# A hybrid encoder block on eight cores: weight loads, sine tables, copies back and norms in another order at the start, and a planner with another model of the queues

## What is computed

```python
h = rmsnorm(x, g_mix)
bc, cc, vc, q, k, va, gc_pre, ga_pre = split(h @ w_in)
y_c = (bc * causal_conv3(cc * vc)) @ w_conv_out
q, k = rope(rmsnorm(q)), rope(rmsnorm(k))
w = softmax(q0 k0 / 8) - lam * softmax(q1 k1 / 8)      # chunk-causal mask, chunks of 64
y_a = (rmsnorm(w @ va) * (1 - lam_init)) @ w_attn_out
x = x + (sigmoid(gc_pre + b) * y_c + sigmoid(ga_pre + b) * y_a) @ w_o
gt, up = split(rmsnorm(x, g_ffn) @ w_gate_up)
x = x + (silu(gt) * up) @ w_down
```

## Time and profile before

| | |
|---|---|
| median of three runs | 2176.37 us (2174.57 to 2176.63) |
| the profiled execution, its own time | 2176.54 us |
| its span on the slowest core (core 0) | 2174.6 us |
| spans of the other cores | 2169.9 to 2173.8 us |
| TensorE matmuls busy | 2135.9 us (98%) |
| VectorE, ScalarE, GpSimd busy | 971.5, 993.3, 408.2 us |
| moved by DMA | 330.97 MB, mean 152 GB/s |

### The profile page before, as it was taken

The page is one execution under the profiler, slowest core; times in us unless marked ns, Lnnn a source line. Parts: engine busy times, 40 slices in busy tenths (PEclk is TensorE's granted clock), DMA queues, the critical chain, the costliest instruction groups (busy, mean ns, idle before and its releaser), DMA issues.

```text
span 2174.6 us, 42940 instructions; the slowest of 8 cores (2169.9 to 2174.6 us)
## 1 busy us (share of the span) xinstructions
PE 2135.9 (98%) x16416; PEld 1289.3 (59%) x16416; DVE 971.5 (45%) x1866; ACT 993.3 (46%) x1545; POOL 408.2 (19%) x488
## 2 busy tenths in 40 slices
PE   6999999999999999999999999999999999999999
PEld 4455444578556585555855558556586565675547
DVE  5874644362465325643256431454323463213532
ACT  4566321123644425445354454644547545557210
POOL 4951110051232003310033000232001220001000
PEclk9999999999999999999999999999999999999999
DMA  9594696547546347553575533745328453252343
GB/s 235 121 208 116 148 218 154 129 103 222 171 126 186 113 143 226 171 152 105 154 215 165 143 104 120 230 123 178 107 79 253 126 166 109 91 184 81 120 171 119
DMA packets 163797, 330.97 MB, mean 152 GB/s; under 512 B 86672, under 2 KB 87568, under 8 KB 163344
## 3 DMA queue, kind: packets, MB, share of 16 engines
q1 hardware_dynamic: 154672, 296.25, 43.7%
q0 software_dynamic: 8928, 31.99, 9.4%
HBM read 291.48 MB, written 49.81 MB: 157 GB/s over the span
## 4 chain that ended last, share of the span: by engine, by line
PE 94%; DVE 2%; DMA 1%; POOL 1%; issue 1%; ACT 1%; SPq 0%; DVEq 0%; POOLq 0%; ACTq 0%
PE psB L1066 28%; PE psB L922 18%; PE psB L1100 14%; PE psO L829 11%; PE psB L796 7%; PE psB L997 5%; PE psB L1038 4%; PE psB L676 4%; PE psB L757 3%; DMA xt<-x 1%; DMA wring<-wblk 0%; PE psB L612 0%; DMA wsc<-wring 0%; DVE h L616 0%; POOL st L705 0%
## 5 line engine op out<-in xcount | busy, mean ns | idle before, releaser
L807 ACT ACTIVATE Pb<-psB 128x1024 bf16<-128x1024 f32 (+1 forms) x544 | 514.3, 995 | 480.9 <-PE psB L796 480.5
L1066 PE MATMUL psB<-h,wring 128*128 128x512 bf16 (+1 forms) x3040 | 625.9, 364 | 2.0 <-DVE kT L1079 1.3
L1066 PEld LDWEIGHTS psB<-h,wring 128*128 128x128 bf16 x3040 | 289.7, 98 | 308.6 <-issue 21.4
L922 PE MATMUL psB<-h,wring 128*128 128x512 bf16 x1792 | 416.9, 381 | 1.9 <-DVE scr L964 1.4
L829 PEld LDWEIGHTS psO<-Vs,Pb 128*128 128x128 bf16 x4224 | 263.5, 98 | 58.9 <-issue 7.8
L829 PE MATMUL psO<-Vs,Pb 128*128 128x129 bf16 x4224 | 290.4, 220 | 2.7 <-ACT Pb L807 2.7
L922 PEld LDWEIGHTS psB<-h,wring 128*128 128x128 bf16 x1792 | 166.6, 98 | 202.7 <-issue 22.3
L1100 PE MATMUL psB<-wring,big 128*128 128x256 bf16 x2464 | 281.4, 273 | 1.9 <-DVE big L1079 1.0
L1075 DVE SCALAR_TENSOR_TENSOR scr<-scr,psB 128x512 f32<-128x512 f32 (+1 forms) x190 | 123.1, 648 | 347.9 <-ACT scr L1073 347.6
L1100 PEld LDWEIGHTS psB<-wring,big 128*128 128x128 bf16 x2464 | 235.7, 98 | 42.2 <-issue 15.1
L1073 ACT ACTIVATE scr<-psB 128x512 f32<-128x512 f32 (+1 forms) x190 | 107.5, 566 | 235.3 <-PE psB L1066 230.8
(11 more groups left out here) (118 smaller groups left out, 1740.5 us busy)
## 6 DMA issues: line engine op xcount, KB each, us to landing
wring<-wsc SPq DMA_DIRECT2D x348, 512.0 KB, 4.3
wring<-wblk POOLq DMA_DIRECT2D x58, 512.0 KB, 8.8
wsc<-wring SPq DMA_DIRECT2D x58, 512.0 KB, 5.3
xt<-x SPq DMA_DIRECT2D x56, 512.0 KB, 7.3
out<-xt SPq DMA_DIRECT2D x28, 512.0 KB, 5.1
wring<-wsc SPq DMA_DIRECT2D x24, 384.0 KB, 3.5
Vs<-x SPq DMA_DIRECT2D x4, 512.0 KB, 20.2
qT<-x SPq DMA_DIRECT2D x4, 512.0 KB, 13.7
```

What stands on the lines that cost most here:

```text
L807: return act_ns(2 * w), [(lambda: A.activation(out=Pb[:, P.slot, :, 0:w], in_=psB[:, a:a + 2, 0:w], func=AF.Exp, scale=0.125), [(S2[0], 0) ...
L922: subs.append((lambda kc=kc: PEE.matmul(bank(B), lhsT=wring[:, W.slot, :].rearrange("p (k c) -> p k c", k=8)[:, kc, col * 128:(col + 1) * ...
L1066: subs.append((lambda kc=kc, gu=gu, B=B: PEE.matmul(bank(B)[:, 0:n], lhsT=wring[:, W.slot, :].rearrange("p (k c) -> p k c", k=8)[:, kc, gu ...
```

## The change

- **Opening.** The first weight block has no wait; the second waits for x's second row block (GATES). The list is V of tile 0, two conv units, V of tile 1 with Q of tile 0 woven into its second half, then the rest of conv with K of tile 0, Q and K of tile 1. So the weight order is V, V, one conv block, Q, Q, and on. Only tile 1's third x load, not its first, waits for the second V block.
- **Tables.** The first table step and the small constants read tile 0's fourth h (`behind`), so VectorE does them after tile 0's norms. The store to `csd` is moved to the first gate unit (soft).
- **Copies back.** Those of the first five blocks come, in the planner's play, after tile 1's fourth x load is in.
- **Tile 2.** Its Squares come, in the planner's play, after activation 18 of tile 1's FFN.
- **PSUM.** psO and psB are one tensor of eight banks. Attention uses banks 6 and 7 where it used psO; bank 6 goes to the free banks when the last attention unit is through.
- **Attention.** `attention` is now `attention_h`; a second form, `attention_q`, by quarters of a tile, is called for tiles from JH = 8 on, which there are none of. The planner's rule for pairs leaves out the condition on P.
- **Planner.** The two DMA queues share the rate 0.35 to 0.65 while both hold work, recomputed at each issue and landing; rate and latency are other constants; a gate unit waits when fewer than two scratch buffers are free, unless it is first in line.

```diff
-LASTW = 0.7
+LASTW, NEARLY = 0.7, 7
+JH, GROUP, FREE, LEAVE = 8, 3, 6, 3
+GATES = {1: (1,)}
...
-    DMA_LAT = 2600.0
+    DMA_RATE = 300.0
+    DMA_LAT = 2200.0
...
+        def rates():
+            both = queue["sp"] and queue["pool"]
+            return {e: self.DMA_RATE * ((0.35 if e == "sp" else 0.65) if both else 1.0) for e in queue}
+
+        def flow(at):
+
+            nonlocal asof
+            r = rates()
+            for e, q in queue.items():
+                if q:
+                    q[0][1] -= r[e] * (at - asof)
+            asof = at
+            for e, q in queue.items():
+                while q and q[0][1] <= 1.0:
+                    t = q.pop(0)[0]
+                    t.land = end = at + self.DMA_LAT
+                    for s in t.succ:
+                        if s.after is not t:
+                            push(end + self.SEM, "dep", s)
+                    for v in t.vals:
+                        push(end + self.SEM, "rel", v)
+
+        def plan_next(at):
+            nonlocal version
+            version += 1
+            r = rates()
+            ends = [q[0][1] / r[e] for e, q in queue.items() if q]
+            if ends:
+                push(at + max(min(ends), 0.01), "flow", version)
 
...
-                            if spare < 3:
+                            if spare < (t.visit[2] if last_kind == "qk" else 3):
                                 continue
                             if last_kind != "qk" and t.next is not None:
                                 t.first = now if t.first is None else t.first
-                                if (spare < 5 or len(self.pools["P"]) < 2 or t.next.ndep > 1) and now < t.first + t.patience:
+                                u, n = t, 1
+                                while n < t.visit[0] and u.next is not None and u.next.ndep <= 1:
+                                    u, n = u.next, n + 1
+                                if (spare < t.visit[1] or n < t.visit[0]) and now < t.first + t.patience:
                                     continue
+                        if t.kind == "gate" and len(self.pools["scr"]) < 2 and t is not line[head]:
+                            continue
...
-                        other = max(f for q, f in dma_free.items() if q != e)
-                        begin = max(dma_free[e], end)
-                        part = self.DMA_RATE * (0.35 if e == "sp" else 0.65)
-                        got = min(t.dma, max(0.0, (other - begin)) * part)
-                        dma_free[e] = begin + got / part + (t.dma - got) / self.DMA_RATE
-                        end = dma_free[e] + self.DMA_LAT
+                        push(end, "issue", t)
+                        for s in t.succ:
+                            if s.after is t:
+                                push(end, "dep", s)
+                        continue
...
-        psO = es.enter_context(nc.psum_tensor("psO", [128, 2, 512], F32))
-        psB = es.enter_context(nc.psum_tensor("psB", [128, NBANK, 512], F32))
+        psB = es.enter_context(nc.psum_tensor("psB", [128, 8, 512], F32))
...
+            behind = [(H[0], 3)]
...
             dve(1250.0, lambda: V.tensor_tensor(
                 out=setup_f, in0=pos_sb[:].unsqueeze(2).to_broadcast([128, 32, 32]),
-                in1=inv.unsqueeze(1).to_broadcast([128, 32, 32]), op=ALU.mult), [C("pos"), C("cst")], KF, pos)
+                in1=inv.unsqueeze(1).to_broadcast([128, 32, 32]), op=ALU.mult), [C("pos"), C("cst")] + behind, KF, pos)
...
-            dma(lambda: nc.sync.dma_start(out=cs_d, in_=cs_all.rearrange("p j s c -> p j (s c)")), VSET, [(CSD, 0)],
-                1048576, pos, lambda: "csd")
...
+        early = []
+
+        def write_back(b, v, n, pos, soft=()):
             dma(lambda: nc.sync.dma_start(out=wsc_d[b][:, 0:n], in_=wring[:, v.slot, 0:n]), [(v, 0)], [(WSC, b)],
-                256 * n, pos + 60000.0, lambda: ("cv", v.slot))
+                256 * n, pos + 60000.0, lambda: ("cv", v.slot), soft=soft)
 
         def weight(p, b):
             if (p, b) in wcur:
                 return wcur[(p, b)]
             v = val("ring")
-            gate = [0] if not wcur else []
+            gate = GATES.get(len(wcur), ())
             wcur[(p, b)] = v
             pos = clk["p"] - 40000.0
             n = 1536 if b in SHORT else 2048
             if p == 0:
                 dma(lambda: nc.gpsimd.dma_start(out=wring[:, v.slot, 0:n], in_=wblk_d[b][:, 0:n]), [(H[0].xs[g], 0) for g in gate], [(v, 0)],
                     512 * n, pos, lambda: ("wc", v.slot), q="pool", strict="w")
-                if b not in HB_AO:
+                if len(wcur) <= NEARLY and b in HB_V + HB_Q + (HB_CONV + 1,):
+                    early.append((b, v, n, pos))
+                elif b not in HB_AO:
                     write_back(b, v, n, pos)
...
-        def norm(X, t, dst, g, pos, pe=True):
+        def norm(X, t, dst, g, pos, pe=True, soft=()):
             XN, SM = val("xn"), val("sm")
-            act(act_ns(1024) + 190.0, lambda: A.activation(out=xn[:, XN.slot, :], in_=xv(X), func=AF.Square,
-                                                           accum_out=sm[:, SM.slot, 0:1]),
-                xk(X), [(XN, 0), (SM, 0)], pos)
+            pl.add("act", act_ns(1024) + 190.0, [(lambda: A.activation(
+                out=xn[:, XN.slot, :], in_=xv(X), func=AF.Square, accum_out=sm[:, SM.slot, 0:1]),
...
-                first = [(weight(0, b), 0) for b in HB_V][1:] if j == 1 and t == 0 else []
+                first = [(weight(0, b), 0) for b in HB_V][1:] if j == 1 and t == 2 else []
                 x_load(X, j, t, pos + step * t - 30000.0, reads=first)
-                norm(X, t, H[j], 0, pos + step * t, j < TN)
+                norm(X, t, H[j], 0, pos + step * t, j < TN, soft)
 
...
+        B6 = pl.val("bank", 6)
+
+        def OB(O, n):
+            return (O, 0) if n else (B6, 0)
...
+                pl.add("pe", w / 512.0 * MM + 15.0, subs, at, hold=False, strict="qk", kind="qk").visit = (2, 5, 3)
...
+        def attention_q(j):
...
+        def attention(j):
+            return attention_h(j) if j < JH else attention_q(j)
...
-        weave(v0 + q0 + v1 + conv0[:4] + conv1[:4], k0 + q1, 16)
-        weave(conv0[4:6] + conv1[4:6] + twins(conv0[6:], conv1[6:], 2), k1, 0, 6)
+        weave(v0 + conv0[:2] + v1 + conv1[:2], q0, 12)
+        for e in early:
+            write_back(*e, soft=[(H[1].xs[3], 0)])
+        weave(conv0[2:6] + conv1[2:6] + twins(conv0[6:], conv1[6:], 2), k0 + q1 + k1, 0, 12)
         a = clk["p"] - 12000.0
         mix0, mix1 = {}, {}
         weave(twins(gate_list(0, 0, HB_GC, HB_CO, by0, mix0), gate_list(1, 0, HB_GC, HB_CO, by1, mix1)), [])
+        dma(lambda: nc.sync.dma_start(out=cs_d, in_=cs_all.rearrange("p j s c -> p j (s c)")), VSET, [(CSD, 0)],
+            1048576, clk["p"] - 10000.0, lambda: "csd", soft=[(mix0[0], 0)])
         dma(lambda: nc.sync.dma_start(out=gb[:], in_=gb_d), [(mix0[0], 0)], [C("gb")], 1048576, clk["p"], lambda: "gb")
...
-        norm_in(2, clk["p"] + 10000.0, 2000.0)
+        norm_in(2, clk["p"] + 10000.0, 2000.0, [(act1[18], 0)])
```

More of the change, by code:

```diff
@@ L1 @@
 import contextlib
+import itertools
 import math
@@ L193, in order @@
         free_at = {e: 0.0 for e in ready}
-        dma_free = {"sp": 0.0, "pool": 0.0}
         now = 0.0
@@ L280, in order @@
                     if t.dma is not None:
-                        other = max(f for q, f in dma_free.items() if q != e)
-                        begin = max(dma_free[e], end)
-                        part = self.DMA_RATE * (0.35 if e == "sp" else 0.65)
-                        got = min(t.dma, max(0.0, (other - begin)) * part)
-                        dma_free[e] = begin + got / part + (t.dma - got) / self.DMA_RATE
-                        end = dma_free[e] + self.DMA_LAT
+                        push(end, "issue", t)
[3 more added lines that the diff above has]
+                        continue
                     for s in t.succ:
-                        if s.after is t and t.dma is not None:
-                            at = now + cost
-                        elif t.eng == "pe" and s.eng == "pe":
+                        if t.eng == "pe" and s.eng == "pe":
                             at = end
@@ L304, in order @@
             while True:
-                if what == "dep":
+                if what == "issue":
+                    flow(now)
+                    queue[x.eng].append([x, float(x.dma)])
+                    plan_next(now)
+                elif what == "flow":
+                    if x == version:
+                        flow(now)
+                        plan_next(now)
+                elif what == "dep":
                     x.ndep -= 1
@@ L627, in build_program, with norm_in @@
         H, HF, QT, TAB, ON = {}, {}, {}, {}, {}
-        def norm_in(j, pos, step):
+        def norm_in(j, pos, step, soft=()):
             H[j] = val("h8")
@@ L801, in qk_exp @@
                 w = 384 if last else 512
```

(4 more changed lines are left out.)

139 lines of the change are left out of this document (124 added, 15 removed).

## The result

| | before | changed |
|---|---|---|
| median of ten runs each | 2176.5 us | 2181.03 us |
| ratio, with its 95% interval | | 1.0024 (1.0014 to 1.0033) |
| the profiled execution, its own time | 2176.54 us | 2183.13 us |
| spans of the eight cores, lowest, median, highest | 2169.9, 2171.8, 2174.6 | 2172.0, 2175.8, 2181.5 |

The change makes the kernel slower by 0.24%, some 5 us; faster had been forecast, by 7.8. The ratios leave disturbed runs out, the medians do not; where both stand, the ratio counts.

The account below looks back on a forecast made before the run. TensorE, busy 2135.9 of 2174.6 us, was taken as the bound, with DMA transfers limiting the opening. Terms −4.8 and −3.0 summed to −7.8, so 2176.54 would become 2168.7 us, range 2161 to 2177.

Parts of the forecast that it names:

- term A: Opening, first V unit: tile 0's V done at about 25 instead of 29.8; −4.8 us, from −6 to −1.5.
- rival 1: Opening: the early weight takes the x blocks' bandwidth, gain falls to −1.5, time 2172.0 us; chance 0.09.
- term B: 30 to 62 us: half of the 5.8 us gaps, which hang on tile 1's norms, go; −3.0, from −7 to +2.
- Tables: Sine table steps from about 20 us: they fit beside the V units; nothing, up to +1 us.
- the rule set against them: Table steps beside tile 1's norms: two-port VectorE steps lock GpSimd out, up to 1.3 us in all; sum left unchanged.
- term C: 62 to 125 us: closer Q/K load on GpSimd set against tile 2's tables not made here; 0, from −3 to +3.
- The lower clock: 30 to 62 us: the 1.2 GHz stretch may not come with fewer gaps, or come elsewhere; no separate size given.
- D1: Held copies back, SP's queue and ring: the copies are hidden behind other work; 0.
- rival 3: Opening: held copies close the ring, the eighth weight block comes late, 15 us of stall, 2183.7 us; chance 0.08.
- D2: Planner's new queue model and rules may change later orders a little; pairs should stay pairs.
- Rival 4: QK pairs in attention: 70 more splits at 0.17 us each cost 12 us, time 2181; chance 0.04.
- Rival 2: Up to 125 us: GpSimd and VectorE are the limit, all but 2 us given back, 2174.5 us; chance 0.09.

Follow-up runs that it names:

- e11: Kernel before with the new weight requests and x loads, the planner's new pair and gate-unit rules and later tile 2 Squares; rest as before: ratio 1.0009.
- e4: Changed kernel with first weight block again behind x's first row block, second free, tile 1's first x load behind the second V block: ratio 1.0067.
- e3: Changed kernel with both the old opening list of units and the old place of the sine table steps: ratio 1.0022.
- e2: Changed kernel with the sine table steps free to run before tile 0's fourth h, as before: ratio 1.0011.
- e1: Changed kernel with the old opening list of units put back, all else as changed: ratio 1.0050.
- e7: Changed kernel, same queue order, VectorE's two rotation products for tiles 0 and 1 cut from 512 to 64 elements: ratio 1.0014.
- e10: Changed kernel, same queue order, with the cuts of e7 and e9 together: ratio 0.9986.
- e15: Changed kernel with tile 2's sines copied on chip by ScalarE (as e14) and the sine table steps in their old place: ratio 1.0002.
- e9: Changed kernel, same queue order, GpSimd's tile 2 table steps read a constant instead of waiting for the table read-back: ratio 1.0017.
- e14: Changed kernel, complete, with tile 2's sines copied on chip by ScalarE instead of read back from the scratch: ratio 1.0017.
- e12: Changed kernel with the planner's old model of the DMA queues (rate 290, latency 2.6 us, one share value): ratio 1.0044.
- e16: Changed kernel with tile 2's sines copied on chip, the sine table steps in their old place and the old opening list: ratio 1.0008.

## Why the prediction was wrong, step by step

- **First V unit (term A, −4.8, bounds −6 to −1.5): −1.6.** The step "nearer to the fastest: I take 11.5" failed. The norm came as worked out (10.28 for 10.2), the weight did not: 12.3 us from issue to use, more than the 10.6 of the median and than its "whole old delay" of 10.5, though nothing else was on its queue until 9.2. And "what follows must hold it" failed with it: x's third block landed 4 us later, and its Square stood another 2 us behind V's copy in ScalarE's queue. The first part is rival 1, which had −1.5 here: the early weight takes x's bandwidth. The Trainium skill (DMA: Bandwidth & Descriptors, "Queues, rings and completion order") says that the engines alternate between the queues packet by packet. By that rule the early weight and x's blocks share the engines, and the landings agree (12.1 us for x's third block, not 8.1). In e11, with the old list, the first 30 us won nothing at all.
- **30 to 62 (term B, −3.0): −2.5.** The size was right, and tile 1's last Square came at 39.37 instead of 44.19, as worked out. It takes all parts together: without the new requests it is at 50.21 (e4), with them but without the held copies at 47.67 (e11), in the runs with both between 38.6 and 41.5. And with the old list the stretch still has 5.3 us idle (e3), 2.9 of them before a transpose of Q. The text had the list as a cost here; it carried part of the gain.
- **Tables (0 to +1): some 3 us.** In idle time it is 1.4 us in 30 to 62 (e2 against the changed kernel). But e2 has the same idle time up to 240 in sum (28.3 and 28.2) and a price of the clock of 1.7 where the changed kernel has 5.1, and it is faster by 0.0013, 2.8 us (the two intervals overlap). The five steps fit beside the V units as said, but they end at 39.4 and GpSimd's table steps after them, and in e1 Q waited for that. Of the rule set against them, one case shows: the power that GpSimd began at 26.29, beside the first table step (26.18), took 1.53 us, where the one at 6.45 took 0.56.
- **62 to 125 (term C, 0): +3.8 of idle.** This is the step that gave the gain back: all kernels with the new list and no work left out have 7.6 to 9.3 us here, where before has 3.9. The text had both halves of it: GpSimd at 92% (57.54 of 63 are 91%), and Q and K "closer together". It then set a favour against them, that tile 2's tables can't be made here. The favour was small (GpSimd 54.2 instead of 57.5 busy), and the load was not GpSimd's alone. Of 63 us, VectorE has 51 and GpSimd 54 in a chain that passes from one to the other and back; sixteen units in 72 us instead of 82 leave it no slack. The square of e1 to e3 shows that this idle time goes with the list, e7 and e10 that it hangs on the chain.
- **The lower clock** was named for 30 to 62 only as something that may go ("it may not come, or come elsewhere"). It came elsewhere: 0.92 in 62 to 125 on core 7, and it had no place in the sum. By the table's account it is most of what makes the change slower and not equal: up to 240 us the idle time is 28.2 in sum against 27.3 before, while the price of the clock is 5.1 against 1.7. It follows the gaps only loosely: e2 and e15 have 8.1 and 8.0 us idle in 62 to 125 and a price of 1.7.
- **The store of the tables (favour of term C; D1: 0): 1.5 us in the changed kernel** (e9 and e14), 2 and 3 us in e2 and e3. The step read the moved store as work taken out of a full stretch. It did not follow the read-back: a DMA of 128 KB that takes 13 us to be of use, and GpSimd's queue behind it.
- **Copies, ring, rival 3 (slower, 0.08): did not happen.** The eighth weight was asked for at 46.80, as predicted (before 48). The ring was no cause.
- **Planner, tile 2's Squares (D2, 0, −3 to +4): +0.8** in 240 to 2150. e12 is slower, so the new queue model is not the cause, and e11, which has the later Squares and the new rule for pairs, has 7.7 there. Rival 4 (split pairs) did not happen either: 24 visits of four QK matmuls before, 26 after, not 70 more. That its 2181 is the measured time is chance.
- **Rival 2 (0.09)** had the mechanism, "earlier matmuls only wait longer in term C", and gave back all but 2 us. What it lacked is that the give-back could exceed the gain: by the clock, and by a second stall further on. No case had that, so nothing above 2177 was in the range but by a mishap. The likeliest case should have been that one: with 98% busy TensorE, and VectorE plus GpSimd at 80 to 90% right behind the opening, a shorter opening was by these rows more likely to be given back than kept.

What stays open: where the +0.8 after 240 comes from, and why gaps of the same sum cost 1.7 us of clock in e2 and 5.1 in the changed kernel. And whether Q and K units begun at 30, as before, with the new gates' x loads, can keep the 2.5 us of 30 to 62: the planner's orders tried (e3, e16, e11) did not.

## What to carry to other kernels

A gap closed ahead of a stretch in which two helper engines are over 80% busy only moves, so cost the next stretch as a chain: number of units, first and last start, time for each. When a store moves later, follow its reader: what waits for the read-back, and what is queued behind that wait. And on eight cores, where the slowest sets the time, allow for a gap to be paid twice where the profile shows TensorE at its lower clock after such gaps.

## What the runs showed that was not expected

- A weight block alone on its queue took 12.3 us from issue to use (2.10 to 14.44), more than the first of the four issued together before (10.5, from 5.36 to its copy back at 15.87).
- A read of 128 KB took 12.9 us (147.37 to 160.23) in one kernel and 13.1 in another (143.02 to 156.11), with the DMA engines busy to 0.94 and 0.89 of these stretches.
- Gaps of 2 to 3 us in TensorE's work were followed by stretches at 1.2 GHz on some cores and not on others of the same run (the price was 1.7 us on cores 0, 2 and 4 of the changed kernel, 3.4 on core 6 and 6.8 on cores 1, 3, 5 and 7). In e10, where the gap of 106 to 110 was gone and 1.8 us of that of 80 to 84 left, none of the eight cores had one in 62 to 125.
- Taking away VectorE work alone, with every queue's order kept, made the kernel before faster by some 3 us. The Q and K chain was a limit in a kernel whose TensorE is 98% busy.
